# Delta rule's inverse: the first five levels as 32-wide diagonal blocks in 32x32 array tiles, the last as a corner product

## The reference, cut to what matters

```python
CHUNK = 64
GDN_HEADS = 4
k_beta = k * beta[..., None]
a_mat = jnp.einsum("bhnid,bhnjd->bhnij", k_beta, k) * decay_strict
eye = jnp.eye(CHUNK, dtype=jnp.float32)
t_inv = lax.linalg.triangular_solve(eye + a_mat, jnp.broadcast_to(eye, a_mat.shape),
                                    left_side=True, lower=True)
u = t_inv @ (v * beta[..., None])
w = t_inv @ (k_beta * jnp.exp(g)[..., None])
def step(state, xs):
    q_c, k_c, u_c, w_c, p_c, gl = xs
    v_new = u_c - jnp.einsum("bhcd,bhde->bhce", w_c, state)
    o = (jnp.einsum("bhcd,bhde->bhce", q_c, state)
         + jnp.einsum("bhij,bhje->bhie", p_c, v_new))
    state = state * jnp.exp(gl)[..., None, None] + jnp.einsum("bhcd,bhce->bhde", k_c, v_new)
    return state, o
```

## Time and profile before

| | us |
|---|---|
| median of 3 runs | 2782.16 |
| lowest and highest | 2778.82 and 2782.26 |
| the profiled execution | 2778.42 |
| its span, first to last instruction | 2776.6 |
| the stretch of the delta rule, first to last product of the inverse | about 471.6 to 611.5 |
| mean granted TensorE clock | 0.985 of full |

### The profile page before, as it was taken

One profiled execution on the slowest core, in us unless ns is written; L12 is line 12 of the kernel. 1 busy time (PEld: TensorE's weight loads), 2 busy tenths in 40 slices (PEclk: granted clock), 3 DMA queues, 4 the chain that ended last, 5 costly groups with the idle time before them and its releaser, 6 DMA issues.

```text
span 2776.6 us, 39285 instructions
## 1 busy us (share of the span) xinstructions
PE 2643.3 (95%) x15530; PEld 2137.2 (77%) x15530; DVE 1879.3 (68%) x2265; ACT 1237.7 (45%) x2316; POOL 408.6 (15%) x354
## 2 busy tenths in 40 slices
PE   7999998999799999999999999899998999999997
PEld 6887566887688888888778888655677888888886
DVE  3466554664687777888974664489646655578889
ACT  3323565332777773333553333467316433343332
POOL 4322001347300000000300000001375000000002
PEclk9999999999999999999999999999999999999999
DMA  3210000004356664332323123411253232343333
GB/s 135 54 38 15 8 6 25 3 21 171 106 168 211 189 198 164 117 121 107 137 91 121 62 91 106 168 60 35 89 196 112 101 111 103 122 164 109 121 106 122
DMA packets 213489, 290.49 MB, mean 105 GB/s; under 512 B 16552, under 2 KB 143807, under 8 KB 213311
## 3 DMA queue, kind: packets, MB, share of 16 engines
q1 hardware_dynamic: 195918, 227.75, 24.8%
q10 hardware_dynamic: 17392, 60.30, 5.5%
HBM read 220.91 MB, written 67.11 MB: 104 GB/s over the span
## 4 chain that ended last, share of the span: by engine, by line
PE 78%; DVE 11%; ACT 4%; POOL 3%; issue 3%; DMA 1%; SPq 0%; ACTq 0%; DVEq 0%; POOLq 0%
PE ps L1739 7%; PE ps L1741 7%; PE ps L1740 7%; PE ps L1794 6%; PE ps L1796 6%; PE ps L1795 6%; PE ps L1877 4%; PE ps L1879 4%; PE ps L1878 4%; PE ps L1530 3%; PE ps L1436 2%; PE ps L1309 1%; PE ps L1311 1%; PE ps L1310 1%; PE ps L1676 1%
## 5 line engine op out<-in xcount | busy, mean ns | idle before, releaser
L1794 PE MATMUL ps<-down_t_hi,down_s_hi 128*128 128x512 f32 x896 | 349.4, 390 | 4.0 <-DVE acc L3332 2.2
L1796 PE MATMUL ps<-down_t_hi,down_s_lo 128*128 128x512 f32 x896 | 348.7, 389 | 0.0
L1795 PE MATMUL ps<-down_t_lo,down_s_hi 128*128 128x512 f32 x896 | 348.6, 389 | 0.0
L2492 ACT CAST down_s_hi<-down_a 128x2048 fp32r<-128x2048 f32 x56 | 107.2, 1915 | 368.7 <-PE ps L1796 327.1
L1142 POOL TENSOR_SCALAR mean_sq<-ssq 128x1 f32<-128x1 f32 x64 | 36.6, 571 | 1294.7 <-ACT squares_junk_ffn L2030 1244.6
L1739 PE MATMUL ps<-act_hi,up_hi 128*128 128x512 f32 (+1 forms) x544 | 205.7, 378 | 6.1 <-issue 2.8
L1740 PE MATMUL ps<-act_lo,up_hi 128*128 128x512 f32 (+1 forms) x544 | 204.9, 377 | 0.0
L1741 PE MATMUL ps<-act_hi,up_lo 128*128 128x512 f32 (+1 forms) x544 | 204.8, 376 | 0.0
L1794 PEld LDWEIGHTS ps<-down_t_hi,down_s_hi 128*128 128x128 f32 x896 | 168.2, 188 | 41.7 <-issue 7.4
L1796 PEld LDWEIGHTS ps<-down_t_hi,down_s_lo 128*128 128x128 f32 x896 | 168.2, 188 | 35.3
L1795 PEld LDWEIGHTS ps<-down_t_lo,down_s_hi 128*128 128x128 f32 x896 | 168.2, 188 | 34.6
(11 more groups left out here) (383 smaller groups left out, 6511.6 us busy)
## 6 DMA issues: line engine op xcount, KB each, us to landing
down_a<-hid_spill SPq DMA_DIRECT2D x32, 1024.0 KB, 6.6
hid_spill<-up_hid ACTq DMA_DIRECT2D x30, 1024.0 KB, 6.2
w_ada<-in_w_ada SPq DMA_DIRECT2D x48, 512.0 KB, 4.0
up_raw<-in_w_in SPq DMA_DIRECT2D x18, 1024.0 KB, 5.1
raw<-in_w_out SPq DMA_DIRECT2D x32, 512.0 KB, 3.7
up_raw<-in_w_up SPq DMA_DIRECT2D x16, 1024.0 KB, 5.6
down_b<-in_w_down SPq DMA_DIRECT2D x16, 1024.0 KB, 6.5
up_raw<-in_w_mlp_in SPq DMA_DIRECT2D x16, 1024.0 KB, 5.3
```

The source lines that it names most:

```text
L1794: pe.matmul(out, ops["s_hi"][:, k, cols], ops["t_hi"][:, k, :], start=first, stop=False, skip_group_check=True)
L1795: pe.matmul(out, ops["s_hi"][:, k, cols], ops["t_lo"][:, k, :], start=False, stop=False, skip_group_check=True)
L1796: mm = pe.matmul(out, ops["s_lo"][:, k, cols], ops["t_hi"][:, k, :], start=False, stop=last, skip_group_check=True)
```

## The change

`t_inv`, `t_inv_T`, `a_level` and `level_y` are kept for levels 0 to 4 as the 32x32 blocks on the diagonal alone: [128 partitions, 4 blocks, 32], half of the elements. Each 64x64 system has two of them, one on partitions 0 to 31 of its half and one on partitions 32 to 63.

- DVE: `gdn_system` gathers the diagonal blocks of `a_T` into a new tile `a_diag`, with two operations over a column mask for each half of the rows (`C_FIRST`, `C_SECOND`), and makes level 0 from it. It had four operations, of 128x256; it has six, two of 128x256 and four of 128x128. The updates of `t_inv_T` and `t_inv` take 128x128.
- TensorE: first turn, y, zt and z of levels 1 to 4 go through `diagonal_products`: 16 matmuls of 32x32, on the four 32x32 tiles on the array's diagonal in turns, in place of eight of 64x64.
- Level 5: the lower left 32x32 corner of the inverse is a product of three blocks. y and zt go through `corner_products`: eight matmuls with 32 rows, 64 columns of weights and 32 moving columns. The first reads `a_T` itself, so POOL makes no `a_level` for it. Of the second only part of the result is wanted; the rest is masked out.
- DVE writes the whole inverse, `t_inv_T_all`, in the last level: two masked copies for each a ahead of `gdn_scaled`, and one masked update for each a behind it, in place of one `t_inv_T` update.
- POOL: 32 masks of 128x128 in place of 40 of 128x256; they wait for `tr0_done` in place of `a_t_done`.
- ACT: the copies out of PSUM take 128x128.
- The order of the steps is as it was. The constants have three more columns; the count at which `level_done` is taken over by a later stage is 32 in place of 40.

```diff
+            def diagonal_products(bank, lhs, rhs, signal):
+                for n in range(GDN_BLOCKS):
+                    for q in range(P // SUB):
+                        rows = slice(q * SUB, (q + 1) * SUB)
+                        mm = pe.matmul(ps[rows, bank, n * SUB:(n + 1) * SUB], lhs(rows, n), rhs(rows, n), start=True, stop=True)
+                mm.then_inc(sem(signal), 1)
+            def corner_products(bank, lhs, rhs, second, signal):
+                for n in range(GDN_BLOCKS):
+                    for g in range(2):
+                        rows = slice(g * CHUNK + second * SUB, g * CHUNK + (second + 1) * SUB)
+                        mm = pe.matmul(ps[gdn_half(g), bank, n * SUB:(n + 1) * SUB], lhs(rows, n), rhs(rows, n), start=True, stop=True)
+                mm.then_inc(sem(signal), 1)
...
-                        block_products(a, lambda h, c, rows, b: m_s[(n + i) % 2][a][rows, b, :],
-                                       lambda h, c, rows, b: t_f[f_old][a][rows, b, :], CHUNK, "y_prod")
+                        if last:
+                            corner_products(a, lambda rows, b: a_t[i % 2][a][rows, b, :], lambda rows, b: t_f[f_old][a][rows, b, :], 0, "y_prod")
+                        else:
+                            diagonal_products(a, lambda rows, b: m_s[(n + i) % 2][a][rows, b, :],
+                                              lambda rows, b: t_f[f_old][a][rows, b, :], "y_prod")
...
+                        if last:
+                            corner_products(a, lambda rows, b: y_s[a][rows, b:b + 2, :].rearrange("p b t -> p (b t)"),
+                                            lambda rows, b: t_r[old][a][rows, b, :], 1, "zt_prod")
+                        else:
+                            diagonal_products(a, lambda rows, b: y_s[a][rows, b, :], lambda rows, b: t_r[old][a][rows, b, :], "zt_prod")
+                            diagonal_products(2 + a, lambda rows, b: t_r[old][a][rows, b, :], lambda rows, b: y_s[a][rows, b, :], "z_prod")
...
-                ch.link(dve.tensor_tensor(tr[:], at[:], each_block(C_LEVEL), ALU.mult))
-                dve.tensor_tensor(tr[:], each_block(C_ID64), tr[:], ALU.subtract).then_inc(sem("tr0_done"), 1)
+                ch.link(dve.tensor_scalar(ad[:], at[:, :, SUB:CHUNK], row_half(C_SECOND), None, ALU.mult))
+                ch.link(dve.scalar_tensor_tensor(ad[:], at[:, :, 0:SUB], row_half(C_FIRST), ad[:], ALU.mult, ALU.add))
+                ch.link(dve.tensor_tensor(tr[:], ad[:], each_diagonal(C_LEVEL), ALU.mult))
+                dve.tensor_tensor(tr[:], each_diagonal(C_ID32), tr[:], ALU.subtract).then_inc(sem("tr0_done"), 1)
...
                     if last:
+                        for a in range(2):
+                            dve.wait_ge(sem("t_done"), 8 * i + 6 + a + 1)
+                            dve.tensor_scalar(t_all[a][:, :, 0:SUB], t_r[old][a][:], row_half(C_FIRST), None, ALU.mult)
+                            ch.link(dve.tensor_scalar(t_all[a][:, :, SUB:CHUNK], t_r[old][a][:], row_half(C_SECOND), None, ALU.mult))
                         gdn_scaled(i, 0)
...
+                            dve.scalar_tensor_tensor(t_all[a][:, :, SUB:CHUNK], diagonal_bank(a), row_half(C_FIRST_NEG),
+                                                     t_all[a][:, :, SUB:CHUNK], ALU.mult, ALU.add).then_inc(sem("t_last_done"), 1)
```

More of the change, by code:

```diff
@@ L354 @@
 C_LEVEL = 640
-C_ID64 = C_LEVEL + CHUNK * len(LEVELS)
-C_CSUM64 = C_ID64 + CHUNK
+SUB = 32
+C_ID32 = 1024
+C_CSUM64 = C_ID32 + CHUNK
 C_KEYCAP = C_CSUM64 + CHUNK
@@ L361 @@
 C_QUARTER_ANGLE = C_QUARTER + 1
-N_CONST = C_QUARTER_ANGLE + 1
+C_FIRST, C_SECOND, C_FIRST_NEG = [C_QUARTER_ANGLE + 1 + n for n in range(3)]
+N_CONST = C_FIRST_NEG + 1
 V_MIXPRE, V_FFNPRE, V_QN, V_KVN, V_CONV = 0, 8, 16, 18, 19
@@ L616, in two_blocks, with diagonals @@
             ("k_w", 25), ("v_b", 29), ("u", 41), ("w_T", 45), ("k_dec", 49), ("o_inter", 53)))
-        e_d, a_t, m_s, t_f = ([blocks(f"{n}{x}_", kb + 2 * x) for x in range(2)]
-                              for n, kb in (("decay", 89), ("a_T", 93), ("a_level", 97), ("t_inv", 101)))
-        t_r = [blocks(f"t_inv_T{x}_", 105 + 2 * x) for x in range(3)]
-        y_s, p_t = blocks("level_y", 111), blocks("p_T", 113)
+        def diagonals(name, kb):
+            return [sb(f"{name}{a}", kb + a / 2, [P, GDN_BLOCKS, SUB]) for a in range(2)]
+        e_d, a_t = ([blocks(f"{n}{x}_", kb + 2 * x) for x in range(2)] for n, kb in (("decay", 89), ("a_T", 93)))
+        a_d, m_s, t_f = ([diagonals(f"{n}{x}_", kb + x) for x in range(2)] for n, kb in (("a_diag", 97), ("a_level", 99), ("t_inv", 101)))
+        t_r = [diagonals(f"t_inv_T{x}_", 103 + x) for x in range(3)]
+        y_s = [sb(f"level_y{a}", 106 + 0.75 * a, [P, GDN_BLOCKS + 1, SUB]) for a in range(2)]
+        t_all, p_t = blocks("t_inv_T_all", 108), blocks("p_T", 113)
         def t_home(i):
@@ L1624, in gdn_pair @@
                     for a in range(2):
-                        pe.wait_ge(sem("level_done"), 10 * i + (2 * (n - 1) + a + 1))
+                        if not last:
+                            pe.wait_ge(sem("level_done"), 8 * i + (2 * (n - 1) + a + 1))
                         if n == 1:
@@ L1639, in gdn_pair @@
                         pe.wait_ge(sem("y_done"), 10 * i + (2 * (n - 1) + a + 1))
-                        block_products(a, lambda h, c, rows, b: y_s[a][rows, b, :],
-                                       lambda h, c, rows, b: t_r[old][a][rows, b, :], CHUNK, "zt_prod")
-                        if not last:
-                            block_products(2 + a, lambda h, c, rows, b: t_r[old][a][rows, b, :],
-                                           lambda h, c, rows, b: y_s[a][rows, b, :], CHUNK, "z_prod")
+                        if last:
[4 more added lines that the diff above has]
+                            diagonal_products(2 + a, lambda rows, b: t_r[old][a][rows, b, :], lambda rows, b: y_s[a][rows, b, :], "z_prod")
                 if more:
@@ L1659, in gdn_pair @@
                                 mm = pe.matmul(ps[:, 2 + g, h * P + c * CHUNK:h * P + (c + 1) * CHUNK], k_w[a][gdn_half(g), 2 * h + c, :],
[L1660 removed]
+                                               t_all[a][gdn_half(g), 2 * h + c, :], start=True, stop=True)
                     mm.then_inc(sem("wu_prod"), 1)
[L1662 removed]
+                    block_products(a, lambda h, c, rows, b: t_all[a][rows, b, :],
                                    lambda h, c, rows, b: v_b[a][rows, b, :], P, "wu_prod")
@@ L3064, in gdn_pair @@
                 gdn_scaled(i, 1)
+            for a in range(2):
+                dve.memset(y_s[a][:, GDN_BLOCKS:, :], 0.0)
             dve.memset(state[0][:], 0.0).then_inc(sem("state_done"), 1)
```

43 lines of the change are left out of this document (26 added, 17 removed).

## The result

| | before | changed |
|---|---|---|
| median of 5 runs, us | 2782.26 | 2800.93 |
| lowest and highest | 2778.82 and 2784.03 | 2794.95 and 2803.38 |
| span of the profiled execution | 2776.6 | 2798.1 |

The ratio is 1.0067, with a 95% interval from 1.0056 to 1.0078. The change makes the kernel 0.67% slower, 18.7 us; forecast were 10 us less. The time is outside the range, and on the other side.

What follows compares the result with a forecast made beforehand. Each level was taken to hang on TensorE through z of tile 0, then DVE's `t_inv` and state. Savings of 3.1 (pair 0), 5.8 (pairs 1 and 2) and 2.1 (pair 3) made 11.0 us, 10 kept: 2772 us, range 2767 to 2787.

Steps and rivals of the forecast that it cites:

- The step that failed: Products on four 32x32 tiles: tiles work at once, so 32 records take 0.26 us against 0.46; this case had chance 0.62.
- The price: Time of one product of 32 records on four 32x32 tiles: 0.26 us, with 0.93 us as the high end.
- straight line over moving columns: From 0.110 us a pair of records at 128 columns and 0.058 at 64, it gives 0.032 us for 32 columns.
- three rivals: Other outcomes: products no faster (2783 us, chance 0.18), a floor for each record (2829, 0.13), the clock falling (2783, 0.07).
- Rival 2: Small products: each record takes its 0.029 us, a product 0.93 us, the kernel 47 us slower at 2829; chance 0.13.
- y, zt and z: Products of levels 1 to 4: y keeps 0.22 us; zt and z of tile 0 save 0.41, less 0.15 in plain levels.
- `o_inter`, DVE's updates and system: Levels: `o_inter` limits y's gain to 0.22 us; updates save 0.13; the system adds 0.4, so levels 2 and 4 keep 0.5.
- The end of a pair: Level 5 and first turns: 0.9 us won in pairs 1 and 2, 0.25 in pair 3, DVE's added copies hidden by slack.
- Pair 0: Pair without state: 3.1 us shorter, from levels 1 and 3 at 0.8 each, y, and first turns.
- Rival 3, the clock: Pairs 1 to 3: thinner TensorE work lets the clock fall to half; 2783 us, up to 2795; chance 0.07.
- a granted clock below 1.00 between 480 and 610: In the delta rule's stretch: named among the signs that would show the prediction wrong.
- The rest of the program: Parts beside the delta rule's stretch: should not move at all.

Runs made afterwards that it cites:

- e1: The kernel before, with each 64x64 matmul of first turns, y, zt and z issued as two of 32 moving columns; 2849.43 us, ratio 1.0251.
- e2: The changed kernel with half of the matmuls in products of levels 0 to 4, each 64 moving columns wide (inverse not right); 2768.16 us, ratio 0.9958.
- e5: The changed kernel without z products and first turns, VectorE turning t_inv_T into t_inv instead; 2776.83 us, ratio 0.9990.
- e6: e5 with level 5's four masked copies moved from VectorE to ScalarE and the level 0 turns put last; 2776.98 us, ratio 0.9984.
- e8: The changed kernel plus eight float32 128x128 matmuls between y and zt of levels 1 to 4, in pair 0 alone; 2800.48 us, ratio 1.0076.
- e3: The kernel before plus three bursts of 384 matmuls (32x32 tiles, then 64x64 with 32 and 64 moving columns) ahead of pair 0's first turns; single run, 2862.88 us.
- e9: e7 with four in place of eight extra matmuls at each of the four places in pair 0; 2771.17 us, ratio 0.9965.
- e7: e6 plus eight float32 128x128 matmuls between y and zt of levels 1 to 4, in pair 0 alone; 2777.88 us, ratio 0.9992.

## Why the prediction was wrong

**The step that failed** is the one that multiplied: "If four tiles keep together as two do, four records take 0.032 us and a product of 32 records 8 x 0.032 = 0.26 us", carried through all levels as if TensorE always had its next instruction. The price was right (0.27 us from product to product), in part by luck: its straight line over moving columns was drawn from 64-wide weights, and there e1 measured no gain at all from 32 columns. What no term held was that the change turns 256 instructions a plain level into 448, and that 448 take 1.75 blocks, 6.5 us at 3.7 us a block, more than the 5.45 of the level before. Over pair 1, 2464 instructions (with prepare, level 5, turns and w_T and u) are 9.6 blocks, 35.6 us, already more than the 34 forecast, and blocks do not come at their best pace through all of it: 40.7. The profile before held the size of a block, in the packets of the instruction queue beside the records counted per line; the prediction did not put the two together. The least distance of two blocks there was 3.7 us, but nothing in it stopped for one, so how fast blocks can come had to be measured. None of the three rivals had it either. Rival 2 was a floor for each record, to be seen in every product; what came is a limit on many products together.

Point by point:

- *y, zt and z.* Right in size wherever a block was at hand: the first level of pair 1, which begins behind a wait of 0.69 us for ScalarE, took 514.96 to 520.91 = 5.95 us, forecast 5.9. The next took 6.38 in place of 4.8, the one after 7.46 in place of 5.9.
- *`o_inter`, DVE's updates and system.* Right, by e2: L1609 0.24 us idle behind `o_inter`, the plain level 4.80, the prepared one 5.84. From the changed kernel's own trace they could not be told. One sum was off: 512.38 + 0.14 is 512.52 and not 512.49, so y wins 0.19 and not 0.22, and 0.19 is what e2 shows (L1593 to L1609 1.91 us, before 2.10 from L1565 to L1581).
- *The end of a pair.* Right in e2, as far as the sum tells, where pairs 1 to 3 are together 8.6 us shorter (7.9 reckoned). Whether VectorE's copies of level 5 are covered in the changed kernel was not tried by itself. In e5 they, or the two turns behind them, were not: e6 takes both away and gains 1.3 us at a pair's end.
- *Pair 0.* Reckoned 3.1 less, 1.9 less in e2, with 10.2 us at half clock in place of 3.4. In the changed kernel it is 8.0 more, and has the largest share of the gaps, 7.5 us, likely since there is no scan in it to put wide matmuls between the small ones; its half clock of 23.9 us may have added to that.
- *Rival 3, the clock.* The sign "a granted clock below 1.00 between 480 and 610" did show (0.69 and 0.98 in the first two stretches). But it was not what cost in pairs 1 to 3: pair 3 of the changed kernel and pair 2 of e8 ran at full clock and still stopped and lost time. For pair 0 its share stays open. Its premise, that the clock follows how much of the time has records, is not what the runs show either: in e3 it was half over 20 us in which TensorE had records all of the time (row below).
- *The rest of the program* did not move, as said: 2168.1 us behind the last w_T product, before 2169.3.

Busy time of e3_bursts in its second burst (granted clock third from the end):

```profile
500.00:520.00 20.00, 20.00 (x380) 20.00 (x380) 0.00 (x0) 0.00 (x0) 0.00 (x0) 0.50 0.01 2
```

## What to carry to other kernels

Count TensorE's instructions as well as its time: two for each record, in blocks of 256 that came at best every 3.3 to 4.0 us here. By these runs a stretch that needs less than some 14.5 ns for an instruction (an estimate, 3.7 us over 256) will be slower than its records say, and splitting matmuls into smaller tiles pays only as far as the count stays under that. Where blocks are 32 wide, a turn on VectorE in place of a second product takes out instructions and array time together: it brought the ratio from 1.0067 to 0.9990 (e5). The 0.35% under the kernel before came only with the further changes of e6 and e9.

## What was not expected of the hardware

- TensorE's instructions arrive 256 at a time, mostly 3.4 to 4.0 us apart in full use, though each transfer itself took only 0.9 to 1.4 us. What fills the rest of the 3.7 us stays open, and so whether another place for the program in memory would shorten it.
- "issue" between two records of one line is the profile's sign of it; the page names no wait for it.
- A float32 record takes the same time for 32 and 64 moving columns where the weights are 64 wide (29 ns on two tiles, and in e1 29 too), and 32x32 weights with 64 moving columns are no quicker (14 ns a record on four tiles, 56 for the four). 32 by 32 on four tiles came to 8.5 to 10 ns a record.
- The granted clock fell to half and stayed there for 54 us in e1 and 68 us in e3, while TensorE ran small matmuls, in e1 one behind the other and in e3 with stops in the first burst alone; eight or four matmuls of 128x128 by 128 columns at each of four places brought half clock in pair 0 down from 20.5 us (e6) to 6.8 (e7, e9). Why is open.
